# One transformer stack in fp32 halves on one Trainium2 core: where the vector engine does the last gate and its rest, the plain updates and the block rests beside the paired down columns

## The reference

```
def swiglu(x, w_gate, w_up, w_down):          # 1024 x 2816, 1024 x 2816, 2816 x 1024
    return (silu(x @ w_gate) * (x @ w_up)) @ w_down
for l in range(2):
    h = h + 0.5 * swiglu(rmsnorm(h, g0), ...)
    h = h + mixer(rmsnorm(h, g1), ...)
    h = h + 0.5 * swiglu(rmsnorm(h, g2), ...)
```

## Time and profile before

| | us |
|---|---|
| median of 3 runs | 3676.91 |
| profiled execution, own time | 3678.66 |
| its span | 3676.6 |
| PE busy in the span | 3598.6 (98%) |
| DVE busy | 2757.8 (75%) |
| ACT busy | 1722.6 (47%) |
| POOL busy | 934.1 (25%) |

### The profile page before, as it was taken

One profiled execution on the slowest core, in us unless ns is written; L12 is line 12 of the kernel. 1 busy time (PEld: TensorE's weight loads), 2 busy tenths in 40 slices (PEclk: granted clock), 3 DMA queues, 4 the chain that ended last, 5 costly groups with the idle time before them and its releaser, 6 DMA issues.

```text
span 3676.6 us, 64756 instructions
## 1 busy us (share of the span) xinstructions
PE 3598.6 (98%) x24230; PEld 3270.6 (89%) x24230; DVE 2757.8 (75%) x3944; ACT 1722.6 (47%) x3001; POOL 934.1 (25%) x757
## 2 busy tenths in 40 slices
PE   8999999999999999999999999999999999999999
PEld 5778888677888889999998999999999999899998
DVE  4677763566777389995667699989998466769997
ACT  3544332345433255554235555555555423646554
POOL 1121110012111025540003035543553000304552
PEclk9999999999999999999999999999999999999999
DMA  3122233212222323332110233232323212032333
GB/s 118 47 75 69 97 97 102 84 47 75 70 97 95 105 86 98 104 99 89 64 64 30 69 103 98 98 110 92 103 93 104 84 58 70 18 104 87 98 98 109
DMA packets 107211, 313.35 MB, mean 85 GB/s; under 512 B 30048, under 2 KB 32224, under 8 KB 106688
## 3 DMA queue, kind: packets, MB, share of 16 engines
q1 hardware_dynamic: 106384, 304.60, 25.7%
q0 software_dynamic: 560, 5.09, 0.4%
HBM read 307.48 MB, written 2.10 MB: 84 GB/s over the span
## 4 chain that ended last, share of the span: by engine, by line
PE 87%; issue 6%; DVE 3%; POOL 2%; ACT 2%; DMA 1%; SPq 0%; POOLq 0%; DVEq 0%; ACTq 0%
PE acc L3155 34%; PE misc L3749 29%; PE acc L3770 5%; PE acc L3324 3%; PE misc L3155 2%; PE misc L4164 1%; PE acc L3666 1%; PE acc L3713 1%; PE acc L3234 1%; POOL probs_hi L2959 1%; PE acc L3864 1%; PE acc L3307 1%; PE acc L3786 1%; PE misc L3941 1%; PE misc L3365 1%
## 5 line engine op out<-in xcount | busy, mean ns | idle before, releaser
L795 ACT CAST w_hi<-stage 128x1024 fp32r<-128x1024 f32 x290 | 303.1, 1045 | 713.8 <-PE acc L3155 584.7
L1690 DVE TENSOR_TENSOR w_lo<-stage,w_hi 128x1024 fp32r<-128x1024 f32 x290 | 396.2, 1366 | 206.2 <-ACT w_hi L795 200.3
L3155 PE MATMUL acc<-x_hi,w_hi 128*128 128x264 f32 (+1 forms) x1984 | 544.3, 327 | 4.2 <-DVE w_lo L1690 3.5
L3155 PE MATMUL acc<-x_lo,w_hi 128*128 128x264 f32 (+1 forms) x1984 | 539.9, 325 | 0.0
L3155 PE MATMUL acc<-x_hi,w_lo 128*128 128x264 f32 (+1 forms) x1984 | 538.2, 324 | 0.0
L2288 DVE TENSOR_TENSOR w_lo<-s_blocks,w_hi 128x512 fp32r<-128x512 f32 x416 | 410.1, 987 | 13.4 <-ACT w_hi L1258 10.2
L2288 DVE TENSOR_TENSOR w_lo<-stage,w_hi 128x512 fp32r<-128x512 f32 (+1 forms) x392 | 352.6, 903 | 38.8 <-ACT w_hi L1258 37.9
L3155 PEld LDWEIGHTS acc<-x_hi,w_hi 128*128 128x128 f32 x1984 | 332.3, 189 | 45.5 <-issue 8.7
L3749 PE MATMUL misc<-t_hi,w_hi 128*128 128x264 f32 x1280 | 367.5, 287 | 1.5 <-ACT u_part L1285 1.5
L3749 PE MATMUL misc<-t_hi,w_lo 128*128 128x264 f32 x1280 | 363.3, 284 | 0.0
L3749 PE MATMUL misc<-t_lo,w_hi 128*128 128x264 f32 x1280 | 362.3, 283 | 0.0
(11 more groups left out here) (495 smaller groups left out, 9202.8 us busy)
## 6 DMA issues: line engine op xcount, KB each, us to landing
stage<-weights SPq DMA_DIRECT2D x568, 512.0 KB, 3.3
rotary_decay<-tables POOLq DMA_DIRECT2D x2, 2048.0 KB, 8.3
x<-x_in SPq DMA_DIRECT2D x4, 512.0 KB, 8.0
lse_rows<-lse_columns SPq DMA_DIRECT2D x128, 0.5 KB, 2.0
rotary_masks<-tables SPq DMA_DIRECT2D x2, 784.0 KB, 4.5
out<-x SPq DMA_DIRECT2D x8, 132.0 KB, 1.9
out<-x SPq DMA_DIRECT2D x8, 124.0 KB, 1.8
params<-params SPq DMA_DIRECT2D x2, 279.0 KB, 3.6
```

The costliest lines, as they stand in the source:

```text
L795: nc.scalar.copy(whi[(p + turn[0]) % 2][:, :], stage[p][:, :]).then_inc(hi_ready, 1)
L1690: nc.vector.tensor_tensor(wlo[w][:, :], stage[p][:, :], whi[w][:, :].bitcast(F32), ALU.subtract).then_inc(lo_ready, 1)
L3155: ins = mm(ps[:, b, 0:tn], ww, act_[:, kt, t0:t0 + tn], start=start and n == 0 and q == 0, stop=stop and n == last and q == 2)
```

## The change

DVE and ACT get another order at the start of each group, and three of the quarter additions change.

- Before the lead tile DVE no longer does `gate_second(b)` and the two `update`s. The block rests that stood behind them move ahead, and the fourth `f_sum_lo` comes after two rests in a row.
- In the lead tile `gate_second(b)` stands after the second block rest, `update` 0 after `ug1`, `f_lo(b)` after `x22`, and `update` 1 after the last addition.
- On ACT `f_hi_of_pair(b)` moves from before the third cast of the lead tile's blocks into the lead tile, between the cast of A22 and the cast of S4, ahead of `u3`.
- In all 24 paired tiles `x11` and `x12` go; in their place `x1` adds the whole first column (528 elements) behind `c12`. `c22` writes over `U3B` instead of `GS`, and `x22` reads `U3B`. So `u3` of the next tile waits for `x22` and not for `c22`, and `c11` and `c12` of the next tile wait for `x1`.

```
@@ pair_steps
-        sums.append(("ug2", b))
+        if j == 2:
+            sums.append(("ug2", b))
...
-            sums += [("c11", n), ("x11", n), ("c22", n), ("ug1", n), ("x22", n), ("c12", n), ("x12", n)]
+            sums += [("c11", n)] + [("ug2", b)] * (n == paired(j)[0])
+            sums += [("c22", n), ("ug1", n), ("x22", n), ("c12", n), ("x1", n)]
@@ ACT, u3
-                        act.wait_ge(pair_sum, sum_at(q, "c22", before(n)))
+                        act.wait_ge(pair_sum, sum_at(q, "x22" if before(n) >= PAIRED else "c22", before(n)))
@@ ACT, the order around a group
                         hi_block()
                         hi_block()
-                        f_hi_of_pair(b)
                         hi_block()
                         ev.up(2)
                         p1(paired(j)[0])
...
                             hi_block()
                             u2(n)
                             hi_block()
+                            if n == paired(j)[0]:
+                                f_hi_of_pair(b)
                             hi_block()
                             u3(n)
@@ DVE, c22 and onto_x
-                    if n >= PAIRED:
-                        dve.wait_ge(pair_sum, sum_at(q, "x11", n))
-                    nc.vector.tensor_tensor(GS[:, 0:HALF] if n >= PAIRED else whole(n)[:, HALF:TALL], banks2(n)[1], U3B[:, :],
+                    nc.vector.tensor_tensor(U3B[:, :] if n >= PAIRED else whole(n)[:, HALF:TALL], banks2(n)[1], U3B[:, :],
                                             ALU.add).then_inc(pair_sum, 1)
...
+                    elif name == "x22":
+                        dve.wait_ge(pair_sum, sum_at(q, "c22", n))
+                        xm, part = x[:, c + 1, HALF:TALL], U3B[:, :]
                     else:
-                        dve.wait_ge(pair_sum, sum_at(q, "c" + name[1:], n))
-                        part = GS[:, HALF:TALL] if name == "x12" else GS[:, 0:HALF]
+                        dve.wait_ge(pair_sum, sum_at(q, "c12", n))
+                        xm, part = x[:, c, :], GS[:, :]
                     nc.vector.scalar_tensor_tensor(xm, part, 0.5, xm, ALU.mult, ALU.add).then_inc(pair_sum, 1)
@@ DVE, the order around a group
                         lo_block()
                         f_sum_lo(0, xh0)
-                        gate_second(b)
                         lo_block()
                         f_sum_lo(1, xh0)
-                        update(KT * j)
+                        lo_block()
                         lo_block()
                         f_sum_lo(3, xh0)
-                        update(KT * j + 1)
-                        lo_block()
                         for n in paired(j):
+                            lead = n == paired(j)[0]
                             c11(n)
                             lo_block()
-                            if n == paired(j)[0]:
-                                f_lo(b)
-                            onto_x("x11", n)
                             lo_block()
+                            if lead:
+                                gate_second(b)
                             lo_block()
                             lo_block()
                             c22(n)
                             lo_block()
                             onto_x("ug1", n)
+                            if lead:
+                                update(KT * j)
                             lo_block()
                             onto_x("x22", n)
+                            if lead:
+                                f_lo(b)
                             c12(n)
                             lo_block()
-                            onto_x("x12", n)
+                            onto_x("x1", n)
+                            if lead:
+                                update(KT * j + 1)
```

More of the change, by code:

```diff
@@ L2322, in c11 @@
                     if RANK2[n]:
-                        dve.wait_ge(pair_sum, sum_at(q, "x22" if before(n) >= PAIRED else "ug1", before(n)))
+                        dve.wait_ge(pair_sum, sum_at(q, "x1" if before(n) >= PAIRED else "ug1", before(n)))
                     nc.vector.tensor_tensor(GS[:, 0:HALF], banks2(n)[2], P1B[:, RANK2[n] % 2, :], ALU.add).then_inc(pair_sum, 1)
@@ L2342, in c12 @@
                     if RANK2[n]:
-                        dve.wait_ge(pair_sum, sum_at(q, "x12" if before(n) >= PAIRED else "ug2", before(n)))
+                        dve.wait_ge(pair_sum, sum_at(q, "x1" if before(n) >= PAIRED else "ug2", before(n)))
                     dve.wait_ge(pair_gate, gate_at(q, "u2", n))
@@ L2352, in onto_x @@
                 def onto_x(name, n):
-                    c = paired_column(n) % KT + (name in ("ug1", "x22"))
-                    xm = x[:, c, 0:HALF] if name in ("x11", "ug1") else x[:, c, HALF:TALL]
+                    c = paired_column(n) % KT
                     if name == "ug1":
                         dve.wait_ge(blk_done, base + PLACE2["A22", n] + 1)
-                        part = banks2(n)[0]
-                    else:
-                        dve.wait_ge(pair_sum, sum_at(q, "c" + name[1:], n))
-                        part = GS[:, HALF:TALL] if name == "x12" else GS[:, 0:HALF]
+                        xm, part = x[:, c + 1, 0:HALF], banks2(n)[0]
+                    elif name == "x22":
+                        dve.wait_ge(pair_sum, sum_at(q, "c22", n))
+                        xm, part = x[:, c + 1, HALF:TALL], U3B[:, :]
+                    else:
+                        dve.wait_ge(pair_sum, sum_at(q, "c12", n))
+                        xm, part = x[:, c, :], GS[:, :]
                     nc.vector.scalar_tensor_tensor(xm, part, 0.5, xm, ALU.mult, ALU.add).then_inc(pair_sum, 1)
```

## The result

| | us |
|---|---|
| before, median of 4 runs | 3677.27 (3676.85 to 3680.53) |
| after, median of 4 runs | 3701.71 (3701.03 to 3703.90) |
| ratio, 95% interval | 1.0066 (1.0048 to 1.0083) |
| profiled execution after, its span | 3703.9, 3701.8 |
| mean granted clock after | 0.994 |

The change costs 24.4 us where 18.4 were forecast. It is slower, as forecast, and by the mechanism forecast; the size lies 0.7 us above the range. The interval of the ratio leaves 1 out, so the loss is clear of the scatter, though it is small. The engines' work hardly moved: the page's part 1 of the kernel after, against the earlier trace rows, has 12 us more of PE, 4 of POOL and 1.5 of DVE.

A forecast was written before the change was run, and what follows sets the result against it. The prediction took DVE, without idle time in the lead tile and shut out by POOL's sums, as the bound. 8 groups x 2.3 = 18.4 us more gave 3695, with an 8-in-10 range of 3684 to 3701.

The forecast's parts named there:

- Step 1: Lead tile: earlier casts and rests let S3 start on PE at 1441.50, 1.22 us won.
- Step 2: POOL asks earlier: the fourth f_sum_lo is shut out and ends 1.12 us later; PE loses 0.4 at A11.
- Step 3: Lead tile, A22: f_hi waits for gate_second and u3 queues behind it; of 1.22 us won, 0.2 is left.
- Step 4: Lead tile: DVE idles 1445.3 to 1446.5, then nearly ties with POOL; POOL first by 0.04 us, S4 0.95 late.
- Step 5: From c22 to the third tile's rest of A11: deferred work adds net 1.0 us, PE is 1.8 late.
- Step 6: Behind A11: nothing won back; small holes in third tile and next chunk, some 0.3 us each; 2.4 a group.
- A: Rival: with u3 before 1444.4 both lead-tile holes go, up to 2.65 us a group, 3656; chance 0.10.
- B: Rival: the debt only moves; PE gains 2.65 us at A22, returns it at the third tile's A11, 3677; chance 0.08.
- C: Rival: DVE wins the lead-tile tie and x1 falls well, 8 x 1.2, 3687; chance 0.17 for 3684 to 3693.
- D: Rival: first sum, tie and small holes at their worst, DVE late into next chunk, 8 x 3.2, 3702; chance 0.10.

The follow-up runs named there:

- e10: Kernel after with gate_second and f_hi_of_pair back where they stood before; updates, f_lo and x1 stay changed: 3683.49 us, ratio 1.0014.
- e2: Kernel before with only the new additions (x1 for x11 and x12, c22 onto U3B), all orders as before: 3684.57 us, ratio 1.0011.
- e9: Kernel after with both updates back behind the second and fourth f_sum_lo, ahead of the lead tile: 3699.93 us, ratio 1.0056.
- e1: Kernel after with ACT's f_hi_of_pair moved behind u3 and the cast that follows it: 3683.71 us, ratio 1.0012.
- e4: Kernel after with x11 and x12 back, c22 onto gate, and f_hi_of_pair behind u3: 3679.59 us, ratio 1.0002.
- e3: Kernel after with x11 and x12 back and c22 onto gate, the new order kept: 3695.87 us, ratio 1.0044.
- e5: Kernel after again, nothing edited, on another chip and against more runs of the kernel before: 3700.43 us, ratio 1.0062.
- e8: Kernel before with a worked-out order of DVE and ACT and c22 onto U3B, x11 and x12 kept: 3662.91 us, ratio 0.9951.
- e11: Exactly the instructions of the kernel before, in another worked-out order of DVE and ACT: 3660.10 us, ratio 0.9950.
- e6: Kernel before with POOL's sums cut to a quarter of their columns, so it computes something else: 3641.01 us, ratio 0.9897.

## Why the prediction was right in kind and short in size

**Step 1, right in size, mistaken in what wins it.** S3 comes 1.22 earlier (1.18 to 1.29 over the groups). The step names the earlier casts first, but e10, which has `gate_second` and `f_hi` back where they stood, has the same 1.22, and e2, with the whole order of before, has 0.00. It is DVE's list that wins it: in e9, e10 and the kernel after the rest of S3 no longer stands behind the fourth `f_sum_lo` and the second `update`.

**Step 2, wrong in its instruction, without effect.** The fourth `f_sum_lo` should have been shut out (2.35) and A11 0.4 late. It took 1.25 and A11 was on time, in all 8 groups. POOL's first sum has its start at 1443.22, ahead of `f_sum_lo` at 1443.58, and yet DVE went first and POOL waited. The shut-outs came later instead, on `gate_second`, which was forecast at its plain 0.42 and took 1.50. So the two errors cancel, which is luck: forecast was `gate_second` to end at 1445.3, and it ended at 1449.65, which is 1445.25 on the clock of before (the first group starts 4.4 later). The Trainium skill, "SBUF — State Buffer", section "Who interferes with whom", says that the one to issue first gets the shared pair. Here the one recorded as first wasn't served first; where page and measurement differ, the measurement decides. In e9 the step comes out as it was forecast: the same `f_sum_lo` took 2.35 in all 8 groups, with POOL's sum ahead of it by the same 0.35 (its rows are in the last section). So the shut-out was no mistake of principle; which of the two is served first could not be read from the rows of before.

**Step 3, right.** `u3` waits for `f_hi`, and A22 is at -0.28 (forecast -0.2). e1 and e10 show it as the cause: without it A22 is at -2.64.

**Step 4, right, tie and all.** DVE idles 1.22 (forecast 1.2), POOL starts 0.02 ahead of the rest (forecast 0.04), and S4 is at +0.89 (+0.95), in all 8 groups.

**Step 5, right in size (+1.81 for +1.8), mistaken in reading.** It was worked out as work added to a stretch that had no room, so the deferred work looked like the cost. e4 defers all the same work and ends at -0.01, since there PE has won at A22 what it gives back. The 1.8 is what the wait of step 3 and the idle time of step 4 took from a DVE that would else have come out even.

**Step 6, right.** The two small holes were forecast at 0.3 each; they are 0.30 (third less A11) and 0.40 (chunk less third). Both belong to `x1`: in e3 and e4, which keep `x11` and `x12`, they are 0.02 at most. `x1` is not dear by its own length. Min, median and longest in ns over the 24 tiles of the kernel after, and below it `x12` of the lead tile before:

```profile
L2364 DVE SCALAR_TENSOR_TENSOR x<-gate,x x24: 694/1791/1802, 1459.8 to 3608.0; 128x528 f32<-128x528 f32 x24
```

```profile
1452.79 1.52 DVE L2361 SCALAR_TENSOR_TENSOR x<-gate,x 128x264 f32<-128x264 f32 x1
```

`x1` is shut out in 16 of 24 tiles, but `x12` was so in 23 of 24 (median 1.51), and only `x11` escaped (0.42). One 1.79 for 0.42 and 1.51 saves DVE a little: it is busy for 2753.8 us in e2 and for 2757.8 before. The cost lies in what the merged addition does to its neighbours, in the two ways that step 6 names. Without `x11` the rests of the third tile come earlier, POOL's fourth sum now starts ahead of the rest in front of `c22`, and shuts it out (1.7 for 0.69, in 7 of 8 groups of e2 and in all 8 of e1 and the kernel after). And `c11` waits for the end of `x1`: it starts 0.6 later (median) for the next chunk, and `u2` behind it. The first of the two, the third tile of group 1 before and in e2:

```profile
1467.61 0.69 DVE L2288 TENSOR_TENSOR w_lo<-stage,w_hi 128x512 fp32r<-128x512 f32 x1
```

```profile
1468.92 1.67 DVE L2288 TENSOR_TENSOR w_lo<-stage,w_hi 128x512 fp32r<-128x512 f32 x1 [0.25 <-ACT w_hi L1258]
```

**The sum, the step that failed.** The steps gave 2.4 a group, and 2.3 was taken for ties that might fall the other way. None did, the second small hole is 0.40 for 0.3, and the groups are at 2.5: 8 x 0.2 = 1.6 of the missing 6.0 us. The second missing term stands nowhere in the prediction, which so put it at nothing: the clock. In 4 of 8 groups PE ran at half clock behind the lead tile's holes; the 8 groups add up to 21.8 where 8 x 2.5 = 20.0, 1.8 us more. The rest, some 2.6, lies outside the groups in code that didn't change; the repeat e5, at 21.6, hasn't got it. So the mis-sized terms of the sum are the 2.3, worth 1.6, and the missing clock, worth 1.5 to 1.8. The remaining 2.6, absent in e5, is taken here for scatter; without it the time would have stood inside the range, near its upper end.

**The rivals.** A (the rests win) needed `u3` before its point, and e1 shows what that gives: 2.64 at A22. But it is no gain at the end, as B says: e4 ends at 0.0. A gain that stays, 2.5 to 2.8 a group, came, with the sums whole, only in e8 and e11, where the additions too have other places. C needed DVE to win the tie of step 4, and POOL won it in all 8 groups. The time falls where D had put it (3698 to 3703, at 0.10), but not for D's reasons: the first sum went the cheap way and a group costs 2.5, not 3.2.

## What to carry to other kernels

An instruction that waits for a full engine must not stand ahead of something that PE needs soon: here one cast on a half-idle ACT made 1.9 of 2.5 us, and to move it behind `u3` gave it back. On an engine without idle time moving work moves only the debt, so look for what makes its instructions long, here POOL, and put the instructions that don't meet POOL where POOL runs. An order worked out in this way, with the same instructions, was worth 20 us (e11), and DVE's busy time fell by 11.0 (2746.8 for 2757.8); how much of it each moved instruction gives was not tried. And merging two operations can cost even where it saves the engine time: `x1` saved DVE 4 us and cost PE 5 in the groups of e2, since another rest then fell under POOL's sum and the next `c11` came later.

## What the runs showed of the hardware

**Half clock behind a long hole.** In the kernel after and in e5 the granted clock halved in 4 of 8 groups each, and in e3 in 6 of 8, each time for 3.4 or 6.8 us, behind PE's hole of 2.2 us (2.9 in e3) ahead of A22 or the following one ahead of S4. In before, e1, e2, e4, e6 to e8, e10 and e11 it did so in no group. Nor in e9, whose holes of the lead tile are 1.7, 1.0 and 1.0 and together no shorter; the windows of e9 over the same two stretches:

```profile
1446.00:1456.00 10.00, 7.30 (x58) 6.88 (x57) 8.68 (x13) 5.17 (x11) 4.21 (x3) 1.00 0.30 105
2624.00:2640.00 16.00, 13.19 (x102) 12.58 (x103) 14.35 (x19) 7.50 (x16) 7.92 (x6) 1.00 0.25 79
```

That the hole brings the fall is seen by this coincidence only; no run varied the hole by itself. Where a fall of 3.4 us met a stretch in which PE waited for DVE anyway it cost 0 to 0.5 us; one of 6.8 cost 1.1 to 1.2 in the kernel after and in e5, and 1.8 in e3.

**Who is served first isn't settled by who started.** In the kernel after, and likewise in e1, e3 to e5, e10 and e11, POOL's first sum starts 0.35 ahead of the fourth `f_sum_lo` and DVE is served first, in all 8 groups. In e9, with the same lead of 0.35 and the same two rests in front, but an `update` instead of an `f_sum_lo` ahead of them, POOL is served first, in all 8 groups:

```profile
1439.22 1.29 DVE L2291 TENSOR_TENSOR w_lo<-s_blocks,w_hi 128x512 fp32r<-128x512 f32 x2
1440.43 2.35 DVE L2380 TENSOR_TENSOR f_sums_lo_second<-f_whole_second,f_sums_hi 128x1056 fp32r<-128x1056 f32 x1
```

```profile
1440.09 1.58 POOL L3099 TENSOR_TENSOR s_blocks<-stage 128x512 f32<-128x512 f32 x1 [8.28 <-DVE w_lo L2291]
```

A longer case is e8, where POOL's sum, from 1441.60, took 2.78 us while DVE, at its second rest by then, ran two further ones at their plain 0.68:

```profile
1440.75 1.28 DVE L2298 TENSOR_TENSOR w_lo<-s_blocks,w_hi 128x512 fp32r<-128x512 f32 x2
1441.95 1.28 DVE L2298 TENSOR_TENSOR w_lo<-stage,w_hi 128x512 fp32r<-128x512 f32 x2
```

```profile
1441.60 2.78 POOL L3096 TENSOR_TENSOR s_blocks<-stage 128x512 f32<-128x512 f32 x1 [9.05 <-DVE w_lo L2298]
```

In the tie of step 4 POOL, 0.02 ahead, won in all 8 groups. What tells the cases apart stays open; no run here was made for it.
